# Transposes moved from the tensor engine to DMA in an eight-core trunk layer

## The reference, cut to what matters

```python
h = rmsnorm(x, norm1_g) * (1 + sc1) + sh1
# token mixer
S, o = gla_recurrence(q, k, v, la, S0)                  # blocks of tokens, a carried 128x256 state for each of 4 heads
o = rmsnorm(o) * gla_norm_g * silu(g);  y_a = o @ w_gla_out
conv = width-3 causal conv of (cc * ch);  y_b = (cb * conv) @ w_conv_out
m = (sigmoid(ga) * y_a + sigmoid(gb) * y_b) @ w_o
x = x + g1 * m
h = rmsnorm(x, norm2_g) * (1 + sc2) + sh2
gt, up = split(h @ w_ffn_in)                            # 1024 -> 2 x 2816
x = x + g2 * ((silu(gt) * up) @ w_ffn_out);  y = rmsnorm(x, norm_f_g)
```

## Time and profile before

| | |
|---|---|
| median of 3 runs | 1441.21 us (1440.6 to 1496.53) |
| the profiled execution: its time | 1442.98 us |
| its span on the slowest core, core 0 | 1441.4 us, granted TensorE clock 0.969 |
| spans of the 8 cores | 1428.5 to 1441.4 us |
| PE busy | 1333.1 us, 92% of the span |
| DVE, ACT, POOL busy | 688.4, 504.3, 109.8 us |
| chain that ended last | PE 74%, ACT 9%, DMA 5%, DVE 5%, issue 5% |
| DMA | 92.66 MB, mean 64 GB/s |

### The profile page before, as it was taken

One profiled execution on the slowest core, in us unless ns is written; L12 is line 12 of the kernel. 1 busy time (PEld: TensorE's weight loads), 2 busy tenths in 40 slices (PEclk: granted clock), 3 DMA queues, 4 the chain that ended last, 5 costly groups with the idle time before them and its releaser, 6 DMA issues.

```text
span 1441.4 us, 22660 instructions; the slowest of 8 cores (1428.5 to 1441.4 us)
## 1 busy us (share of the span) xinstructions
PE 1333.1 (92%) x7660; PEld 695.5 (48%) x7660; DVE 688.4 (48%) x1257; ACT 504.3 (35%) x1122; POOL 109.8 (8%) x208
## 2 busy tenths in 40 slices
PE   1577999998989899889999999999999999999997
PEld 1333445444545455544445555555555445555443
DVE  1467557543656577642233334962122552212486
ACT  1576456432445455431211112981111001111233
POOL 3000100000000000011110120010000002000000
PEclk9778999998999999999999999999999999999999
DMA  9736401206211111154342366532223006222222
GB/s 173 212 117 154 52 9 30 52 2 59 51 23 23 23 23 23 23 96 73 52 74 38 62 102 135 179 68 37 40 35 44 1 1 103 36 40 35 59 103 110
DMA packets 42797, 92.66 MB, mean 64 GB/s; under 512 B 5206, under 2 KB 8166, under 8 KB 42684
## 3 DMA queue, kind: packets, MB, share of 16 engines
q0 software_dynamic: 29264, 53.02, 24.9%
q1 hardware_dynamic: 13420, 38.20, 8.2%
HBM read 133.95 MB, written 10.25 MB: 100 GB/s over the span
## 4 chain that ended last, share of the span: by engine, by line
PE 74%; ACT 9%; DMA 5%; DVE 5%; issue 5%; POOL 0%; ACTq 0%; DVEq 0%; SPq 0%; POOLq 0%
PE psum L464 72%; ACT sb_arena L447 6%; DMA sb_wring<-wfm 2%; DVE sb_arena L450 2%; PE psum L467 2%; ACT sb_tmpB L447 2%; DMA sb_wring<-w_in 1%; ACT sb_rstd L447 1%; DMA sb_wring<-w_mod 1%; DVE sb_arena L454 1%; DVE sb_arena L458 1%; DMA sb_arena<-xm 1%; DVE sb_tmpB L458 0%; POOL sb_wring L437 0%; DVE sb_arena L455 0%
## 5 line engine op out<-in xcount | busy, mean ns | idle before, releaser
L464 PE MATMUL psum<-sb_arena,sb_wring 128*128 128x384 bf16 (+3 forms) x4448 | 837.5, 347 | 11.5 <-DVE sb_arena L461 10.1
L464 PEld LDWEIGHTS psum<-sb_arena,sb_wring 128*128 128x128 bf16 x4448 | 430.1, 98 | 385.3 <-issue 44.2
L464 PE MATMUL psum<-sb_wring,sb_arena 128*128 128x512 bf16 (+2 forms) x1596 | 350.4, 378 | 4.3 <-DMA sb_wring<-w_in 4.3
L447 ACT ACTIVATE sb_tmpB<-psum 128x384 f32<-128x384 f32 (+1 forms) x264 | 139.6, 532 | 606.3 <-PE psum L464 576.1
L450 DVE TENSOR_TENSOR sb_arena<-psum,sb_tmpB 128x384 bf16<-128x384 f32 (+5 forms) x254 | 148.6, 587 | 324.6 <-PE psum L464 306.1
L464 PEld LDWEIGHTS psum<-sb_wring,sb_arena 128*128 128x128 bf16 (+1 forms) x1596 | 155.8, 99 | 184.0 <-issue 7.4
L437 POOL DMA_DIRECT2D sb_wring<-wfm x140 | 75.3, 545 | 912.5 <-PE psum L464 769.0
L450 DVE TENSOR_TENSOR sb_tmpB<-psum,sb_tmpB 128x384 f32<-128x384 f32 (+2 forms) x80 | 47.8, 598 | 171.0 <-PE psum L464 170.5
L450 DVE TENSOR_TENSOR sb_arena<-psum,sb_arena 128x512 f32<-128x512 f32 (+2 forms) x106 | 72.6, 685 | 35.3 <-PE psum L464 35.1
L447 ACT ACTIVATE sb_arena<-sb_arena 128x1024 bf16<-128x1024 f32 (+2 forms) x60 | 60.5, 1010 | 76.7 <-DVE sb_arena L450 61.8
L467 PE MATMUL psum<-sb_identb,sb_arena 128*128 128x128 bf16 (+2 forms) x636 | 58.4, 234 | 24.6 <-DVE sb_arena L454 22.1
(11 more groups left out here) (94 smaller groups left out, 582.3 us busy)
## 6 DMA issues: line engine op xcount, KB each, us to landing
sb_wring<-wfm POOLq DMA_DIRECT2D x140, 256.0 KB, 6.1
sb_arena<-xm SPq DMA_DIRECT2D x29, 512.0 KB, 5.5
sb_arena<-xp SPq DMA_DIRECT2D x16, 512.0 KB, 8.2
ym<-sb_arena SPq DMA_DIRECT2D x16, 512.0 KB, 2.7
sb_wring<-w_ffn_out POOLq DMA_DIRECT2D x22, 256.0 KB, 4.6
sb_wring<-w_in POOLq DMA_DIRECT2D x16, 256.0 KB, 9.7
sb_wring<-w_mod POOLq DMA_DIRECT2D x16, 256.0 KB, 7.8
sb_wring<-w_o POOLq DMA_DIRECT2D x8, 256.0 KB, 8.0
```

The costliest lines, as they stand in the source:

```text
L447: return P.op("act", lambda e: e.activation(out=out, in_=in_, func=func, **kw), reads=reads, writes=writes)
L464: return P.op("pe", lambda e: e.matmul(out, lhsT=lhsT, rhs=rhs, start=start, stop=stop), reads=reads, writes=writes)
```

## The change

`gla_C` becomes one DMA transpose on SP's queue, from `ogb` straight into `ogT`: no PE transposes, no PSUM bank, no DVE copy. In the projection stage `scale` moves from DVE to ACT and is followed by a DMA transpose into `h2T` on SP's queue; `post` now works on a whole column group, three steps after its last tile (the last group: in step 18), and does the modulation in place in `h2T`, all on DVE. New regions `r_h2r` stand for the unmodulated rows. FFN pieces are taken in steps 8, 11, 14, 17 and 18 instead of 17 and 18, and the FFN's first half begins with groups 0 to 3 of blocks 0 and 1, then group 4 of both. The x loads go to POOL's queue, behind `w_o`, and the first two FFN weights are issued after the sixth of them. In `conv_gen`, `taps(4)` is written right after `taps(3)`, one `yield` earlier.

```diff
+        def dmat(out, in_, reads, writes):
+            return P.op("sp", lambda e: e.dma_start_transpose(out=out, in_=in_), reads=reads, writes=writes, dma=True)
...
         def gla_C(t):
             c0, R = tile_cols(t)
             oi = gst[t]["og"]
-            bT = mbank()
-            for k in range(KT):
-                tr(psb(bT)[:, k * 128:k * 128 + R], ogb[oi][0:R, k * 128:(k + 1) * 128], identb[0:R, 0:R], [r_ogb[oi], r_identb], [r_ps[bT]])
-            cp(ogT[:, :, c0:c0 + R], psb(bT).rearrange("p (k r) -> p k r", k=KT)[:, :, 0:R], [r_ps[bT]], [r_og[t]])
+            dmat(ogT[:, :, c0:c0 + R], ogb[oi][0:R, :], [r_ogb[oi]], [r_og[t]])
...
                 for g in range(4):
                     cu(g)
-                    cx, r_cx = taps(g)
+                    tp = taps(g)
+                    if g == 3:
+                        tp4 = taps(4)
                     yield
-                    cv(g, cx, r_cx)
-                    if g == 3:
-                        cx, r_cx = taps(4)
+                    cv(g, *tp)
                     yield
-                cv(4, cx, r_cx)
+                cv(4, *tp4)
                 yield
...
             def scale(t):
                 R = tile_cols(t)[1]
                 xi, gi = st[t]
-                ts(xv[xi][0:R, :], xres[0:R, t, :], rstd[0:R, gi * 4:gi * 4 + 1], None, ALU.mult, None, r_xres[t] + [r_rstd[gi]], [xg[xi]])
-
-            def post(t):
...
+                c0 = tile_cols(t)[0]
+                act(xv[xi][0:R, :], xres[0:R, t, :], AF.Copy, r_xres[t] + [r_rstd[gi]], [xg[xi]], scale=rstd[0:R, gi * 4:gi * 4 + 1])
+                dmat(h2T[:, :, c0:c0 + R], xv[xi][0:R, :], [xg[xi]], [r_h2r[t]])
+
+            def post(g):
+                c0, n = GRP[g]
+                np_ = n if g < NG - 1 else n - 64
+                runs = [(0, np_, 0)] + ([] if g < NG - 1 else [(np_, 32, 1), (np_ + 32, 32, 2)])
+                for k in range(KT):
+                    for (co, nn, seq) in runs:
+                        v = h2T[:, k, c0 + co:c0 + co + nn]
+                        ts(v, v, modT[:, 3, k, seq:seq + 1], modT[:, 2, k, seq:seq + 1], ALU.mult, ALU.add,
+                           [r_h2r[t] for t in GTILES[g]] + [r_modT[3], r_modT[2]], [r_h2[k][g]])
 
             for t in range(19):
                 if t < 17:
                     proj(t)
-                else:
+                if t in (8, 11, 14, 17, 18):
                     next(filler)
                 if 0 <= t - 1 < 17:
                     scale(t - 1)
-                if 0 <= t - 2 < 17:
-                    post(t - 2)
                 if t < 17:
                     stats(t)
+                for g in range(NG):
+                    if t == min(GTILES[g][-1] + 3, 18):
+                        post(g)
                 yield
...
+            order = [(j, g) for j in range(11) for g in range(NG)]
+            if part == 0:
+                order = [(j, g) for j in range(2) for g in range(NG - 1)] + [(0, NG - 1), (1, NG - 1)] + order[2 * NG:]
...
+        wo = [wrow(w_o[k * 128:(k + 1) * 128, :]) for k in range(KT)]
+        f1w = {}
         for t in range(17):
             R = 128 if t < NPT else 64
-            dma("sp", xres[0:R, t, :], x_src(t), [], r_xres[t])
-        wo = [wrow(w_o[k * 128:(k + 1) * 128, :]) for k in range(KT)]
-        f1 = ffn1_gen(0)
+            dma("pool", xres[0:R, t, :], x_src(t), [], r_xres[t])
+            if t == 5:
+                f1w[0] = (wfm("f1", 0), wfm("f1", 22))
+        f1 = ffn1_gen(0, f1w)
```

More of the change, by code:

```diff
@@ L268, in build, with raw_regs @@
         r_hTh = mreg("hTh", [(A0 + (k * TX + TM) * 2, A0 + (k * TX + TX) * 2) for k in range(KT)], "hT")
+        def raw_regs(name, off, width, cols, grp_):
+            return [mreg("%s_%d" % (name, i), [(off + (k * width + c0) * 2, off + (k * width + c0 + n) * 2) for k in range(KT)], grp_)
+                    for i, (c0, n) in enumerate(cols)]
         xres = view(A0, 17 * 4096, F32).rearrange("p (n d) -> p n d", d=D)
@@ L284, in build @@
         r_h2 = fm_regs("h2", B0, KT, TM, GRP, "h2")
+        r_h2r = raw_regs("h2r", B0, TM, CH, "h2r")
         nfg = view(B0, 4096, F32)
@@ L1115, in scale @@
                 xi, gi = st[t]
-                ts(xv[xi][0:R, :], xres[0:R, t, :], rstd[0:R, gi * 4:gi * 4 + 1], None, ALU.mult, None, r_xres[t] + [r_rstd[gi]], [xg[xi]])
-            def post(t):
[L1119 to L1130, removed]
-                            i_ = psb(b)[:, kk * 128 + co:kk * 128 + co + nn]
-                            rr = [r_ps[b], r_modT[3], r_modT[2]]
-                            if on_act:
-                                act(o_, i_, AF.Identity, rr, [r_h2[k][g_]], scale=modT[:, 3, k, seq:seq + 1], bias=modT[:, 2, k, seq:seq + 1])
-                            else:
-                                ts(o_, i_, modT[:, 3, k, seq:seq + 1], modT[:, 2, k, seq:seq + 1], ALU.mult, ALU.add, rr, [r_h2[k][g_]])
+                c0 = tile_cols(t)[0]
[10 more added lines that the diff above has]
+                           [r_h2r[t] for t in GTILES[g]] + [r_modT[3], r_modT[2]], [r_h2[k][g]])
             for t in range(19):
@@ L1144, in wo_gen, with ffn1_gen @@
                     scale(t - 1)
-                if 0 <= t - 2 < 17:
-                    post(t - 2)
                 if t < 17:
                     stats(t)
+                for g in range(NG):
+                    if t == min(GTILES[g][-1] + 3, 18):
+                        post(g)
                 yield
-        def ffn1_gen(part):
-            for j in range(11):
-                jj = part * 11 + j
-                w1, w2 = wfm("f1", jj), wfm("f1", 22 + jj)
-                for g, (c0, n) in enumerate(GRP):
+        def ffn1_gen(part, ws=None):
+            ws = {} if ws is None else ws
+            order = [(j, g) for j in range(11) for g in range(NG)]
+            if part == 0:
+                order = [(j, g) for j in range(2) for g in range(NG - 1)] + [(0, NG - 1), (1, NG - 1)] + order[2 * NG:]
+            for j, g in order:
+                jj = part * 11 + j
+                if j not in ws:
+                    ws[j] = (wfm("f1", jj), wfm("f1", 22 + jj))
+                w1, w2 = ws[j]
+                c0, n = GRP[g]
+                if True:
                     bg = newbank()
```

## The result

The changed kernel took 1446.84 us (median of 5 runs), the kernel before beside it 1441.0. The ratio is 1.0045 [1.0028, 1.0063], 6.5 us slower. In some executions of either kernel the cores of one die run several per cent longer at a lower clock; the ratios leave these out, the medians don't. Forecast were 19 us less, so the time lies outside the range of 1402 to 1442. The profiled execution took 1450.11 us; its slowest core was core 3, with a span of 1448.6.

A forecast was written before the change was run, and what follows sets the result against it. PE, busy 92% of the span, was taken as the bound. Gains of 10.0 us (projection) and 9.3 (attention) sum to 19.3, giving 1422 us against the median of 1441.21, range 1402 to 1442.

The forecast's parts named there:

- The bound: Whole kernel: PE, busy 92% of the span, bounds it; gains are PE time removed or PE waits shortened.
- The attention stage: Attention stage: transposes off PE 6.1 us, tail 1.5, two stalls 0.7, seventh channel 1.0; gain 9.3 us.
- The taps: Attention stage, conv: earlier taps(4) gains 0.7 us over two stalls and about 1.0 in the seventh channel.
- the stalls at cu(4): Attention stage: two PE stalls of 4.17 and 4.11 us stay, each 0.35 us shorter.
- the third: Attention stage, seventh channel: PE's stall of 3.35 us at 602.74 gets about 1.0 us shorter.
- The size of a transpose: Projection stage: one row tile's DMA transpose takes 1.5 us of the engines, between 0.8 and 3.0.
- The step that failed: Projection stage, first group: late early transposes cost nothing; DVE's step comes about 911 us, PE has four tiles of lead.
- Slower: Rival, projection stage: transposes above 3.7 us each on SP's queue block DVE and PE; 1470 and up, chance 0.12.
- Shared engines: Rival, projection stage: transposes at 3.0 us each beside x and weights erase the gain; 1430 to 1442, chance 0.14.
- Covered: Projection stage's end: the 9 us chain to the last group hides behind 13.9 us of PE pieces.
- The half clock: Attention stage: PE runs at half clock after each cu(4) stall, so each stall costs 7 us.
- The 10.0 us of the stage: Projection stage gain: 7.4 us of transposes off PE plus 2.6 of waits and DVE's slower beat.

The follow-up runs named there:

- a1: Kernel before with only the attention-stage DMA transposes and the new taps order, projection stage as before: 1429.0 us, ratio 0.9917.
- b3: a1 with the conv taps in their old order, taps(4) after cv(3): 1430.3 us, ratio 0.9923.
- b1: Changed kernel with x loads issued from SP's queue, six tiles ahead, in turn with the transposes: 1438.4 us, ratio 0.9969.
- a4: Changed kernel without the x loads, the add taking the projection's own product twice: 1432.2 us, ratio 0.9940.
- c2: Changed kernel, x in turn on SP's queue, modulation blocks first, fourth group's step later, (1,0) before (0,3), four more FFN pieces before the last group: 1432.6 us.
- d1: c2 with the last group's step three pieces later on DVE and the fourth group's a tile earlier: median 1430.3 us, ratio 0.9898 (1426.7 us by ratio).

## Why the prediction was wrong

**The bound, right.** PE sets the span; each wait of it and each stretch at the lower clock shows in the time.

**The attention stage, right in kind and a little low.** Forecast 9.3 us; a1 gave 12.0 by its ratio [9.7 to 14.3], the first part of the profiled runs 11. The transposes cost nothing on SP, as argued. The taps gave 1.3 us by b3's time and 1.6 by the stalls, where 1.7 were forecast: the stalls at cu(4), which stayed as forecast, lost 0.5 us each instead of 0.35, and the third 0.6 instead of 1.0. Where the remaining 2 or 3 us come from I can't say, as the waits for `w_mod` vary by more than that from core to core.

**The size of a transpose, right,** though 1.5 was a pick between bounds of 0.8 and 3.0. It took 1.54 us of the engines beside x (1.3 without), and 17 of them fit beside x, as b1 shows.

**The step that failed** is "early transposes will be late, but the DVE step that needs tile 3's comes about 911 us and PE has four tiles of lead behind it". The date was sound: 911 is 24.1 us after PE's first projection matmul in the kernel before, and DVE came to the step 25.9 us after it (873.46 to 899.4). All of this stage starts earlier in the changed kernel, the x loads too: the first goes out 2.1 us ahead of that matmul, where it was 2.5 in the kernel before. Wrong were the two other parts. First, how late: I counted full engines as a matter of bytes, 1.5 us more per tile. In the trace the transposes of tiles 1 and 2 hold their queue for 11.0 and 11.2 us beside x in the other queue, so that tile 3's goes out at 909.6 and the step starts at 914.90, 15.5 us after DVE was ready. Second, the lead: four tiles is what the banks hold, but I had put the first piece that reads the step's result two tiles behind it, so PE had 6.9 us of work and then stood for 10.76, waiting for the step itself. That is close to the rival "Slower" (the step blocks DVE, and PE stands), with the price of the engines of "Shared engines"; but PE waited for the step, not for evictions. The rival had it decide from 3.7 us on SP's queue for all 17 transposes. Two of the first four were far above that and most of the others below, so the loss was 17 us and not 90. This collision is worth 11 to 13 of the 17.4 us (b1, a4).

**"Covered", wrong by two terms.** After tile 16 the chain to the last group was reckoned at 9 us, with PE's 13.9 us of pieces as cover. In the changed kernel it took 17.9 (955.37 to 973.22). The fourth group's step, 3.9 us, stood ahead of tile 16's evictions on DVE, which started 4.9 us after tile 16's matmuls and took 2.9 instead of 1.5; tile 16's transpose took 5.3 us with its wait for the queue, not 2.5. PE's pieces too took longer than 13.9, with waits and the lower clock, so its first wait there was only 0.3 us. The second term was the step itself. Eight operations of 384 columns were put at 3.8 us and took 3.9, so that size was right; but the last group has 24 operations, not eight, since its tile 16 holds two sequences, and each of 32 columns costs 0.39 to 0.42 us too. That is 10.1 us where I had 3.8: 1.29 us a block, in which PE has one matmul of 0.35 to 0.53 us to do. More cover alone did little (c2): the waiting step on DVE holds the evictions, and eight banks are four pieces. With the step later in DVE's order as well, the wait went (d1).

**The half clock** was counted for the stalls of the kernel before, and in no rival's price. It was about 7.9 of the 27.7 us found on core 3.

**The 10.0 us of the stage, 2 to 3 too high.** In d1 PE of core 3 stands for 1.7 us together between its first projection matmul and 980, and the second part gained 6.0. With them gone it would be 7.7, about the 7.4 of the transposes on PE. The 2.6 us of waits and beat that I added on top didn't come. That would close the last 3 us of the account above; no run isolates it, and the second parts of the kernel before alone differ by 2 us from core to core.

## What to carry to other kernels

A transfer that is small in bytes is not small in time beside bulk loads in another queue. What helped here was to issue these a few tiles ahead, in turn with the latency-bound transfers and in their queue. Take the landing time under load, not alone, into the sum. Where two lists are mixed, count the lead from the step to the first work that reads its result, not to the last free bank. Where a change puts an operation with a far-off dependence into an in-order engine's list, ask first which evictions stand behind it and how many banks they free; more work for the bound engine alone didn't cover that, together with a later place in the list it did.

## What the runs showed of the hardware

- A DMA transpose of 128 by 1024 bf16 holds SP's queue for 1.22 us when the engines have little else to do (attention stage; 1.23 in a4) and lands in 2.7 to 4.5 us. Beside the x loads on POOL's queue two of them held it for 11.0 and 11.2 us, and one landed after 25.8. The Trainium skill's 1309 ns for a 128x128 block ("VectorE: DVE Perf Modes", The three transpose paths) would be 10.5 us for the eight as an estimate; measured are 1.54 us of the engines beside x. The Trainium skill's other figure, 261 GB/s ("DMA: Bandwidth & Descriptors", Latency and other measured facts), gives 1.0 us as an estimate and was the nearer.
- An in-place tensor_scalar on bf16 in SBUF takes DVE 413 ns for 512 columns, 383 for 384 and 294 for 32, and one of 32 columns follows its like after 0.39 to 0.42 us: almost all of it is a fixed cost.
- After long waits PE was granted the lower clock for a while: 0.89 and 0.82 in the windows behind 10.8 and 6.6 us of waiting in the changed kernel, and 1.00 still on core 7 of d1, with a wait of 1.5 us. In the changed kernel that added about 0.4 us for each us of waiting.
